# The experts' gather and scatter on GpSimd: one loop over blocks, with the next gather issued between a scatter and the wait for its landing

## The chip, the cores and the metric

The kernel runs on one core of one Trainium2 chip. The metric is the device time of one execution in microseconds. Three runs of the kernel before are shown, and one further execution was profiled. The engines are called by the profile's names: PE is TensorE, DVE is VectorE, ACT is ScalarE, POOL is GpSimd, SP is SyncE, which issues the plain transfers.

## The reference, cut to what matters

One layer of a streaming encoder runs on 1024 prompt tokens and 32 sample tokens: a combined projection, two attention branches, gates, an output projection and a layer norm. Then comes the part that is changed, a mixture of experts with 32 experts, of which each token takes two:

```python
dest = pad_start[e_s] + jnp.arange(n_assign) - cnt_start[e_s]
xb = jnp.zeros((n_blocks * MOE_BLOCK, h.shape[1]), h.dtype).at[dest].set(h[tok_s])
block_e = jnp.minimum(jnp.searchsorted(pad_end, jnp.arange(n_blocks) * MOE_BLOCK, side='right'), N_EXPERTS - 1)

def expert_block(a):
    xblk, e = a
    return (jax.nn.silu(xblk @ lp['w_gate'][e]) * (xblk @ lp['w_up'][e])) @ lp['w_down'][e]

yb = lax.map(expert_block, (xb.reshape(n_blocks, MOE_BLOCK, -1), block_e)).reshape(n_blocks * MOE_BLOCK, -1)
return jax.ops.segment_sum(yb[dest] * w_s[:, None].astype(yb.dtype), tok_s, num_segments=n_tok)
```

The assignments are sorted by expert and cut into blocks of 128 rows of one expert. The matrices of one expert are 1024 x 512 (gate), 1024 x 512 (up) and 512 x 1024 (down).

## The kernel before, in words

**Tiling.** After the router has counted, the program knows how many blocks each expert has. Every expert gets at least one, so that the code can walk the experts in order; with these inputs there are 40 blocks, eight of them second blocks of an expert. Each block is 128 rows of 1024 numbers. Float32 products are made of three matmuls on split operands (high by high, low by high, high by low), and each operand is split into a high part (ACT rounds it) and a rest (DVE subtracts).

**One block on PE** (`block_mm`, lines 1017 to 1050): gate and up for the first half of the hidden width, then for the second (L1030 to L1032); then `turn_x(b + 1)`, eight transposes of the **next** block's rows `xg` into PSUM (L1008); then the down product of this block (L1046 to L1048). `turn_x` waits for the gather: `x_got` must be `16 * b + 16`.

**The weights.** SP loads each expert's weights in six transfers of 1 MB, each as soon as the last block of the expert before has used that part (`w_used`). ACT rounds them (L1325) and DVE makes the rest (L1823). Both do it in thirds, in a fixed order between the small steps of a block. On ACT the order at a new expert is: first third, `drain_y` (L1318, two copies of the previous block's result from PSUM to `yb`), second third, and so on. `drain_y` waits for the end of the down product and for the semaphore `give_step`.

**POOL** carries the data that depend on the routing. Both helpers issue an indirect transfer:

- `fetch(b)` gathers block b's rows into the single buffer `xg`. It reads the block's column number (`value_load`), waits until the gather before has landed and until `turn_x(b - 1)` has emptied `xg` (`xb_tr`), writes a one-element tick (`step`, L2051), copies 128 row numbers into `idx` (L2060), ticks again and issues (L2063). The ticks order instructions that depend on each other through semaphores.
- `give(b)` scatters the result of block b - 1 from the single buffer `yb` to `y_rows`. It copies 128 destinations (L2075), waits for `drain_y` (`y_read`), ticks (`settle`, L2070), issues (L2079), **waits until the scatter has landed** (`y_sent`), and ticks again. This second tick raises `give_step`, which lets ACT's next `drain_y` overwrite `yb`.

The loop goes over experts: `fetch(b + 1)`, `give(b)`, and then an inner loop with the same pair for further blocks of the expert. Since an engine works in order, `fetch` of the next round is not reached until the scatter of this round has landed. Both transfers use the software-driven DMA queue q0; SP's transfers use q1.

After the last block POOL issues the last `give`. SP then waits for all scatters (`y_sent`), reads the rows back, and a second layer norm ends the program.

Of the kernel before, what the change touches and what calls it, by code (L numbers as in the profile page):

```python
# [14 lines left out]
ALU = mybir.AluOpType  # L15
# [4 lines left out]
I32 = mybir.dt.int32  # L20
U32 = mybir.dt.uint32

P = 128
# [11 lines left out]
NE, NG, EPG = 32, 4, 8  # L35
DE = 512
MAXBLK = NE + 2 * LIVE // P
# [101 lines left out]
NTL = NT + 1  # L139
# [30 lines left out]
def build(nc, io):  # L170
    with ExitStack() as ctx:
        def sem(name):
            return ctx.enter_context(nc.semaphore(name))
# [26 lines left out]
        ps = ctx.enter_context(nc.psum_tensor("ps", [P, 8, 512], F32))  # L200
# [14 lines left out]
        r = Region(base)  # L215
# [3 lines left out]
        r = Region(work)  # L219
# [12 lines left out]
        r = Region(rope_at)  # L232
# [13 lines left out]
        r = Region(work)  # L246
# [15 lines left out]
        def u_at(c):  # L262
            return nc_u + c * TOK * 4
# [7 lines left out]
        r = Region(u_at(C_KA))  # L271
        back = [r.take("back0", [P, 2, LIVE])]
        assert r.at <= u_at(C_QB)
        r = Region(work)
# [5 lines left out]
        r = Region(base)  # L280
# [4 lines left out]
        r = Region(base + 2 * 4 * KD * D)  # L285
# [4 lines left out]
        r = Region(nc_u)  # L290
# [16 lines left out]
        r = Region(after_m)  # L307
# [31 lines left out]
        total = r.take("total", [P, NE])  # L339
        reach = r.take("reach", [P, NE])  # L340
        blk = r.take("blk", [P, 4])
        blk_i = r.take("blk_i", [1, 2, MAXBLK + 1], I32)
        last_blk = r.take("last_blk", [1, NE], I32)
        rank = r.take("rank", [P, NTL, 2])
        spare = r.take("spare", [P, 1])
# [2 lines left out]
        r = Region(base)  # L348
        e_raw, e_hi, e_lo = map(list, zip(*[r.split(f"we{n}", [P, GC]) for n in range(2)]))
        assert r.at <= nc_u  # L350
        r = Region(work)
# [3 lines left out]
        r = Region(moe_small)  # L355
# [14 lines left out]
        r = Region(ring_at)  # L370
        pad = r.take("pad", [P, NCOL])
        rank_f = r.take("rank_f", [P, NCOL])
        r = Region(ring_at + 2 * 4 * NCOL)
        dest = r.take("dest", [P, NCOL], I32)

        r = Region(base)
        yg = [r.take(f"yg{n}", [P, 2, D]) for n in range(YB)]
        on = [r.take(f"on{n}", [P, D]) for n in range(2)]
        r = Region(work)
# [6 lines left out]
        def s(name):  # L386
            if name not in sems:
                sems[name] = sem(name)
            return sems[name]
# [1016 lines left out]
        def _(dve):  # L1406
# [419 lines left out]
            for t in range(NTL):  # L1826
# [20 lines left out]
                if t == 7:  # L1847
# [37 lines left out]
                                     op1=ALU.add).then_inc(s("blk_done"), 1)  # L1885
            rest_third(0, 0, range(2))
            dve.wait_ge(s("blk_tr"), 1)
            dve.tensor_copy(blk_i[:, 0, :], ps[0:1, 1, 0:MAXBLK + 1]).then_inc(s("plan"), 1)
            dve.tensor_scalar(blk_i[:, 1, :], ps[0:1, 1, P:P + MAXBLK + 1], float(NE * NTL - 1), None, ALU.min
                              ).then_inc(s("plan"), 1)  # L1890
            rest_third(0, 0, range(2, 4))

# [59 lines left out]
            with dve.Fori(1, NE) as e:  # L1952
                b = dve.value_load(last_blk[0:1, bass.ds(e - 1, 1)], min_val=0, max_val=MAXBLK - 2) + 1
# [3 lines left out]
            nb = dve.value_load(last_blk[0:1, NE - 1:NE], min_val=NE - 1, max_val=MAXBLK - 1) + 1  # L1957
            dve.wait_ge(s("w_used2"), nb * 2)
            for t in ORDER:
                M = rows_of(t)  # L1960
                last = dve.tensor_scalar(share[0:M, t, 0:M], ident[0:M, 0:M], prow[0:M, t, 1:2], None, ALU.mult)
# [41 lines left out]
        def _(pool):  # L2003
# [9 lines left out]
            for dst, src in ((ident_r, ident), (mask_r, blkmask)):  # L2013
                last = pool.tensor_copy(dst[:], src)
# [33 lines left out]
            def step(count):  # L2048

                pool.wait_ge(s("pool_step"), count)  # L2050
                pool.tensor_tensor(tick[:, 0:1], zero[0:1, :], zero[0:1, :], ALU.add).then_inc(s("pool_step"), 1)  # L2051

            def fetch(b, first):

                if not first:
                    column = pool.value_load(blk_i[0:1, 1, bass.ds(b, 1)], min_val=0, max_val=NE * NTL - 1)
                    pool.wait_ge(s("x_got"), 16 * b)
                    pool.wait_ge(s("xb_tr"), b)
                    step(2 * b)
                    pool.tensor_copy(idx[:, 0:1], tokens[:, bass.ds(column, 1)]).then_inc(s("idx_set"), 1)  # L2060
                pool.wait_ge(s("idx_set"), b + 1)
                step(2 * b + 1)
                pool.indirect_dma_start(out=xg[:], out_offset=None, in_=h_rows,  # L2063
                                        in_offset=bass.IndirectOffsetOnAxis(ap=idx[:, 0:1], axis=0)
                                        ).then_inc(s("x_got"), 16)

            def settle(count):

                pool.wait_ge(s("give_step"), count)
                pool.tensor_tensor(tick[:, 1:2], zero[0:1, :], zero[0:1, :], ALU.add).then_inc(s("give_step"), 1)  # L2070

            def give(done):

                column = pool.value_load(blk_i[0:1, 1, bass.ds(done - 1, 1)], min_val=0, max_val=NE * NTL - 1)
                pool.tensor_copy(idx[:, 1:2], dest[:, bass.ds(column, 1)]).then_inc(s("idx_out"), 1)  # L2075
                pool.wait_ge(s("idx_out"), done)
                pool.wait_ge(s("y_read"), 2 * done)
                settle(2 * done - 1)
                pool.indirect_dma_start(out=y_rows, out_offset=bass.IndirectOffsetOnAxis(ap=idx[:, 1:2], axis=0),  # L2079
                                        in_=yb[:], in_offset=None).then_inc(s("y_sent"), 16)  # L2080
                pool.wait_ge(s("y_sent"), 16 * done)
                settle(2 * done)

            def more_blocks(e, b):
                last = pool.value_load(last_blk[0:1, bass.ds(e, 1)], min_val=0, max_val=MAXBLK - 1)
                with pool.If(last > b):
                    with pool.Fori(b + 1, last + 1) as more:
                        fetch(more + 1, False)
                        give(more)

            fetch(0, True)
            pool.wait_ge(s("tokens"), 1)
            pool.wait_ge(s("plan"), 3)
            fetch(1, False)
            pool.wait_ge(s("dests"), 1)
            more_blocks(0, 0)
            with pool.Fori(1, NE) as e:
                b = pool.value_load(last_blk[0:1, bass.ds(e - 1, 1)], min_val=0, max_val=MAXBLK - 2) + 1
                fetch(b + 1, False)
                give(b)  # L2100
                more_blocks(e, b)
            nb = pool.value_load(last_blk[0:1, NE - 1:NE], min_val=NE - 1, max_val=MAXBLK - 1) + 1

            give(nb)

            for j in range(NTL):
                v = mv[j % 2][0:rows_of(ORDER[j])]
# [93 lines left out]
```

## Time and profile before

| | us |
|---|---|
| median of three runs | 1733.33 |
| lowest and highest | 1728.21 and 1743.21 |
| the profiled execution | 1728.43 |
| its span, first to last instruction | 1726.6 |

| engine | busy us | share of the span |
|---|---|---|
| PE | 1665.7 | 96% |
| DVE | 1099.2 | 64% |
| ACT | 824.2 | 48% |
| POOL | 317.3 | 18% |

The experts take from about 934 us to 1675 us. Busy shares are means over the whole span, so the work around the change is read from windows between two starts of `turn_x`, one per block. The mean granted clock of the span is 0.983.

### The profile page before, as it was taken

To read this page: it belongs to the slowest core of one execution; us is meant where nothing else is said; L and a number is where in the kernel's file an instruction comes from. 1 tells how busy PE (TensorE), PEld (TensorE's weight loads), DVE (VectorE), ACT (ScalarE), POOL (GpSimd) and SP (SyncE) were. 2 spreads that over 40 slices of the span, in tenths; PEclk is the share of its full clock that TensorE was granted. 3 is DMA by queue.
4 is the path that set the end of the run, shared out by engine and by line. 5 is a ranking of instruction groups with operands and counts; after the bars stand their busy time and mean duration, and the time that the engine had idled before them with its cause. 6 is when DMAs were issued, how large, how long until landed. Compare 5 with 4: busy or idle time off the path is not lost. (4 is left out here: it accounts for less than half of the span.)

```text
span 1726.6 us, 28243 instructions
## 1 busy us (share of the span) xinstructions
PE 1665.7 (96%) x9680; PEld 1390.1 (81%) x9681; DVE 1099.2 (64%) x1719; ACT 824.2 (48%) x1291; POOL 317.3 (18%) x383
## 2 busy tenths in 40 slices
PE   8999999999999999999996999999999999999986
PEld 8988888788888889998874778888878888887762
DVE  3466655455555454553578874559886568698867
ACT  3134443433434334111222764458785557587853
POOL 0000000000000000002431332223343223233431
PEclk9999999999999998999996999999999999999998
DMA  5110010411111112533225976669997668899967
GB/s 194 37 44 26 26 37 13 175 44 41 50 50 51 50 47 109 190 129 109 78 93 189 366 266 233 262 247 391 408 398 280 252 255 331 330 399 408 395 224 283
DMA packets 64332, 324.19 MB, mean 188 GB/s; under 512 B 7681, under 2 KB 14465, under 8 KB 37601
## 3 DMA queue, kind: packets, MB, share of 16 engines
q1 hardware_dynamic: 52592, 280.68, 42.7%
q0 software_dynamic: 11664, 42.47, 7.0%
q8 instruction: 52, 0.85, 0.2%
q14 instruction: 24, 0.19, 0.0%
HBM read 280.36 MB, written 42.76 MB: 187 GB/s over the span
## 5 line engine op out<-in xcount | busy, mean ns | idle before, releaser
L1823 DVE TENSOR_TENSOR we_lo<-we_raw,we_hi 128x1024 fp32r<-128x1024 f32 x384 | 449.4, 1219 | 31.8 <-ACT we_hi L1325 27.9
L1325 ACT ACTIVATE we_hi<-we_raw 128x1024 fp32r<-128x1024 f32 x384 | 378.0, 1052 | 44.1 <-issue 39.3
L1030 PE MATMUL ps<-we_hi,xb_hi 128*128 128x512 f32 x640 | 256.7, 401 | 3.4 <-DVE xb_lo L1904 2.0
L1032 PE MATMUL ps<-we_hi,xb_lo 128*128 128x512 f32 x640 | 250.8, 392 | 0.0
L1031 PE MATMUL ps<-we_lo,xb_hi 128*128 128x512 f32 x640 | 249.7, 390 | 0.0
L554 PE MATMUL ps<-xT_hi,win_hi 128*128 128x358 f32 (+1 forms) x432 | 145.4, 337 | 8.3 <-DVE win_lo L1423 8.3
L1030 PEld LDWEIGHTS ps<-we_hi,xb_hi 128*128 128x128 f32 x640 | 120.5, 188 | 34.9 <-DVE we_lo L1823 9.4
L1032 PEld LDWEIGHTS ps<-we_hi,xb_lo 128*128 128x128 f32 x640 | 120.4, 188 | 26.3
L555 PE MATMUL ps<-xT_lo,win_hi 128*128 128x358 f32 (+1 forms) x432 | 141.5, 327 | 0.0
L556 PE MATMUL ps<-xT_hi,win_lo 128*128 128x358 f32 (+1 forms) x432 | 141.1, 327 | 0.0
L1031 PEld LDWEIGHTS ps<-we_lo,xb_hi 128*128 128x128 f32 x640 | 120.8, 189 | 23.6
L845 PE MATMUL ps<-xT_hi,wgate_hi 128*128 128x352 f32 x384 | 135.9, 354 | 0.5 <-DVE wgate_lo L1582 0.5
L1046 PE MATMUL ps<-we_hi,hb_hi 128*128 128x512 f32 x320 | 136.1, 425 | 0.0
L1048 PE MATMUL ps<-we_hi,hb_lo 128*128 128x512 f32 x320 | 126.7, 396 | 0.0
L1047 PE MATMUL ps<-we_lo,hb_hi 128*128 128x512 f32 x320 | 126.2, 394 | 0.0
L847 PE MATMUL ps<-xT_hi,wgate_lo 128*128 128x352 f32 x384 | 125.2, 326 | 0.0
L846 PE MATMUL ps<-xT_lo,wgate_hi 128*128 128x352 f32 x384 | 125.1, 326 | 0.0
L2070 POOL TENSOR_TENSOR tick<-const 1x1 f32<-1x1 f32 x80 | 45.8, 573 | 332.9 <-DMA y_rows<-yb,idx 243.8
L1898 DVE TENSOR_TENSOR hid<-sg,ps 128x256 f32<-128x256 f32 x80 | 33.5, 418 | 101.2 <-ACT sg L1329 101.2
L1197 ACT ACTIVATE wt<-ps 128x768 f32<-128x768 f32 (+2 forms) x60 | 47.9, 799 | 94.4 <-PE ps L776 93.8
L1560 DVE TENSOR_TENSOR_SCAN left<-keep 128x384 f32<-128x384 f32 (+5 forms) x66 | 51.5, 821 | 64.2 <-ACT keep L1185 33.5
L554 PEld LDWEIGHTS ps<-xT_hi,win_hi 128*128 128x128 f32 x432 | 81.9, 189 | 9.1 <-DVE win_lo L1423 8.0
(343 smaller groups left out, 3233.7 us busy)
## 6 DMA issues: line engine op xcount, KB each, us to landing
we_raw<-w_moe SPq DMA_DIRECT2D x192, 1024.0 KB, 7.3
win_raw<-w_u SPq DMA_DIRECT2D x18, 512.0 KB, 3.5
gates<-sgt SPq DMA_DIRECT2D x48, 176.0 KB, 1.8
back<-gates SPq DMA_DIRECT2D x8, 1056.0 KB, 5.9
wgate_raw<-w_mix SPq DMA_DIRECT2D x16, 512.0 KB, 3.6
yg<-y_rows SPq DMA_DIRECT2D x8, 1024.0 KB, 8.8
xT_raw<-xT SPq DMA_DIRECT2D x8, 536.0 KB, 8.3
kvb<-U SPq DMA_DIRECT2D x1, 4224.0 KB, 15.6
```

Of the source, the lines that this page charges most:

```text
L554: pe.matmul(o, whi[n][:, kk, :], xh[:, kk, a:b], start=kk == 0, stop=False)
L555: pe.matmul(o, whi[n][:, kk, :], xl[:, kk, a:b], start=False, stop=False)
L556: return pe.matmul(o, wlo[n][:, kk, :], xh[:, kk, a:b], start=False, stop=kk == KD - 1)
L845: pe.matmul(o, ghi[c % 2][:, k, :], xh[:, k, cols], start=k == 0, stop=False, skip_group_check=True)
L1030: pe.matmul(o, xb_hi[:, k, :], e_hi[half][:, c], start=k == 0, stop=False)
L1031: pe.matmul(o, xb_hi[:, k, :], e_lo[half][:, c], start=False, stop=False)
L1032: last = pe.matmul(o, xb_lo[:, k, :], e_hi[half][:, c], start=False, stop=k == KD - 1)
L1046: pe.matmul(o, hb_hi[:, k, :], e_hi[2][:, cols], start=k == 0, stop=False)
L1047: pe.matmul(o, hb_hi[:, k, :], e_lo[2][:, cols], start=False, stop=False)
L1048: last = pe.matmul(o, hb_lo[:, k, :], e_hi[2][:, cols], start=False, stop=k == 3)
L1325: act.activation(e_hi[n][:, c], e_raw[n][:, c], ACT.Copy).then_inc(s("d_hi" if n == 2 else "e_hi"), 1)
L1823: dve.tensor_tensor(e_lo[n][:, c], e_raw[n][:, c], as_f32(e_hi[n][:, c]), ALU.subtract).then_inc(s("d_split" if n == 2 else "e_split"), 1)
```

## The change

POOL's two nested loops become one loop over blocks. `give` is cut in two: the part up to the issue keeps its name, and the wait for the landing with its tick is called `given`. `fetch(2)` moves ahead of the loop, and inside the loop `fetch(b + 2)` stands between the two parts. At the end one gather more is issued than before (`fetch(nb + 1)`), for which the table of columns gets one entry more. Nothing is changed on PE, ACT and SP, and on DVE only the width of two copies of that table (49 columns to 50).

```diff
-            dve.tensor_copy(blk_i[:, 0, :], ps[0:1, 1, 0:MAXBLK + 1]).then_inc(s("plan"), 1)
-            dve.tensor_scalar(blk_i[:, 1, :], ps[0:1, 1, P:P + MAXBLK + 1], float(NE * NTL - 1), None, ALU.min
+            dve.tensor_copy(blk_i[:, 0, :], ps[0:1, 1, 0:MAXBLK + 2]).then_inc(s("plan"), 1)
+            dve.tensor_scalar(blk_i[:, 1, :], ps[0:1, 1, P:P + MAXBLK + 2], float(NE * NTL - 1), None, ALU.min
                               ).then_inc(s("plan"), 1)
...
                 settle(2 * done - 1)
                 pool.indirect_dma_start(out=y_rows, out_offset=bass.IndirectOffsetOnAxis(ap=idx[:, 1:2], axis=0),
                                         in_=yb[:], in_offset=None).then_inc(s("y_sent"), 16)
+
+            def given(done):
+
                 pool.wait_ge(s("y_sent"), 16 * done)
                 settle(2 * done)
-
-            def more_blocks(e, b):
-                last = pool.value_load(last_blk[0:1, bass.ds(e, 1)], min_val=0, max_val=MAXBLK - 1)
-                with pool.If(last > b):
-                    with pool.Fori(b + 1, last + 1) as more:
-                        fetch(more + 1, False)
-                        give(more)
 
             fetch(0, True)
             pool.wait_ge(s("tokens"), 1)
             pool.wait_ge(s("plan"), 3)
             fetch(1, False)
             pool.wait_ge(s("dests"), 1)
-            more_blocks(0, 0)
-            with pool.Fori(1, NE) as e:
-                b = pool.value_load(last_blk[0:1, bass.ds(e - 1, 1)], min_val=0, max_val=MAXBLK - 2) + 1
-                fetch(b + 1, False)
+            fetch(2, False)
+            nb = pool.value_load(last_blk[0:1, NE - 1:NE], min_val=NE - 1, max_val=MAXBLK - 1) + 1
+            with pool.Fori(1, nb) as b:
                 give(b)
-                more_blocks(e, b)
-            nb = pool.value_load(last_blk[0:1, NE - 1:NE], min_val=NE - 1, max_val=MAXBLK - 1) + 1
-
+                fetch(b + 2, False)
+                given(b)
             give(nb)
+            pool.wait_ge(s("x_got"), nb * 16 + 32)
+            step(nb * 2 + 4)
```

POOL's instructions in the loop over experts before, from a scatter's issue (`DMA y_rows`) onward; `y_sent` counts landed scatters:

```order
L2079 DMA y_rows<-yb,idx 2240x1024
L2081 REGISTER_ALU
L2070 TENSOR_TENSOR tick<-const 1x1 [waits give_step,y_sent]
L2085 ISA
L2085 TENSOR_LOAD last_blk
L2085 ISA x2
L2086 COMPARE_AND_BRANCH
L2087 UNCONDITIONAL_BRANCH
L2087 ISA
L2056 TENSOR_LOAD blk_i
L2056 ISA x2
L2057 ISA
```

The tick that waits for the landing stands two rows behind the issue; the branches of the two loops and the load of the next gather's column come after it.

The same place in the changed loop, from the scatter's issue to the second tick ahead of the gather; `xb_tr` counts emptied `xg` buffers:

```order
L2079 DMA y_rows<-yb,idx 2240x1024
L2056 ISA
L2056 TENSOR_LOAD blk_i
L2056 ISA x2
L2057 ISA
L2050 REGISTER_ALU [waits xb_tr,x_got]
L2051 TENSOR_TENSOR tick<-const 1x1 [waits pool_step]
L2060 ISA
L2060 COPY idx<-tokens 128x1
L2061 REGISTER_ALU
L2050 REGISTER_ALU [waits idx_set]
L2051 TENSOR_TENSOR tick<-const 1x1 [waits pool_step]
```

Between the scatter and the gather's own instructions no wait for `y_sent` is left; what POOL waits for here is `xb_tr`.

The rows that follow in the changed loop, from the gather's issue (`DMA xg`) to the head of the next round:

```order
L2063 DMA xg<-h_rows,idx 128x1024
L2084 REGISTER_ALU
L2070 TENSOR_TENSOR tick<-const 1x1 [waits give_step,y_sent]
L2094 ISA
L2094 COMPARE_AND_BRANCH
L2074 ISA
L2074 TENSOR_LOAD blk_i
```

The tick that waits for the landing, and that ACT's `drain_y` waits for, now stands behind the gather's issue, and one branch closes the loop.

## Rows read from the trace of the kernel before

**Rows 1.** The page, chain that ended last, its shares of the span by line:

```profile
PE ps L1030 7%; PE ps L1032 7%; PE ps L1031 7%; PE ps L1046 4%; PE ps L1048 3%; PE ps L1047 3%; DMA xg<-h_rows,idx 2%; PE ps L1008 2%; PE ps L1014 1%; POOL y_rows L2079 1%; DMA y<-on 1%; POOL idx L2060 0%; POOL tick L2070 0%; DVE on L1988 0%; DVE yg L1979 0%
```

**Rows 2.** Waits of PE and POOL: who for whom, total us, times, longest:

```profile
PE ps L1008 <- DMA xg<-h_rows,idx: 10.2, 6, 3.3
...
POOL tick L2070 <- DMA y_rows<-yb,idx: 243.8, 40, 9.2
...
POOL tick L2051 <- issue: 81.3, 25, 19.5
POOL tick L2051 <- PE ps L1008: 73.8, 16, 5.9
```

**Rows 3.** Windows between `turn_x` starts: us, busy of PE PEld DVE ACT POOL, PEclk, DMA:

```profile
987.90:1009.56 21.66, 18.34 (x85) 14.40 (x83) 19.29 (x22) 15.53 (x22) 7.75 (x8) 0.99 0.99 381
1009.56:1029.06 19.50, 19.47 (x84) 15.90 (x85) 13.81 (x16) 14.18 (x19) 5.61 (x9) 0.93 0.66 253
...
1209.00:1227.16 18.16, 18.16 (x85) 14.55 (x84) 16.50 (x19) 14.85 (x21) 7.03 (x8) 1.00 1.01 411
...
1245.30:1265.11 19.81, 18.34 (x86) 14.41 (x84) 17.43 (x21) 15.52 (x22) 8.66 (x8) 1.00 1.01 411
...
1590.20:1609.54 19.34, 18.30 (x85) 14.41 (x84) 17.00 (x21) 15.53 (x22) 8.67 (x8) 1.00 1.01 404
1609.54:1628.30 18.76, 18.33 (x85) 14.56 (x85) 16.19 (x18) 14.73 (x20) 7.75 (x8) 1.00 0.98 384
1628.30:1649.04 20.74, 18.35 (x84) 14.53 (x85) 18.32 (x21) 14.98 (x21) 7.86 (x8) 1.00 1.01 389
```

**Rows 4.** Timeline of POOL, 1237 to 1260 us: start, duration, instruction, [idle before]:

```profile
1237.60 2.03 POOL L2079 DMA_INDIRECT y_rows<-yb,idx  x1 [0.16 <-POOL tick L2070]
1248.47 0.36 POOL L2070 TENSOR_TENSOR tick<-const 1x1 f32<-1x1 f32 x1 [8.84 <-DMA y_rows<-yb,idx]
1251.02 1.16 POOL L2051 TENSOR_TENSOR tick<-const 1x1 f32<-1x1 f32 x1 [2.19 <-issue]
...
1254.61 1.81 POOL L2063 DMA_INDIRECT xg<-h_rows,idx  x1 [0.15 <-issue]
...
1258.23 1.81 POOL L2079 DMA_INDIRECT y_rows<-yb,idx  x1 [0.16 <-POOL tick L2070]
```

**Rows 5.** Timeline of PE, the transposes of three blocks:

```profile
933.66 1.97 PE L1008 MATMUL ps<-const,xg 128*128 128x128 f32 x8 [1.57 <-DMA xg<-h_rows,idx]
...
1209.00 1.03 PE L1008 MATMUL ps<-const,xg 128*128 128x128 f32 x8
...
1265.11 1.09 PE L1008 MATMUL ps<-const,xg 128*128 128x128 f32 x8 [1.47 <-DMA xg<-h_rows,idx]
```

**Rows 6.** Timeline of POOL, a gather that the transposes released, 1030 to 1034 us:

```profile
1030.33 1.13 POOL L2051 TENSOR_TENSOR tick<-const 1x1 f32<-1x1 f32 x1 [4.34 <-PE ps L1008]
...
1033.40 1.00 POOL L2063 DMA_INDIRECT xg<-h_rows,idx  x1 [0.47 <-issue]
```

**Rows 7.** Timeline of ACT, `drain_y` of the block at 1209 us:

```profile
1217.31 1.06 ACT L1318 ACTIVATE yb<-ps 128x512 f32<-128x512 f32 x2
```

**Rows 8.** The gather's line: issue durations, min/median/max ns; issue to landing:

```profile
L2063 POOL DMA_INDIRECT xg<-h_rows,idx x41: 986/1553/2032, 929.0 to 1658.4; - x41
...
DMA to landing us min/median/max: 4.2/6.5/10.7
```

**Rows 9.** Timeline of POOL, the last two scatters, 1662 to 1680 us:

```profile
1662.02 1.80 POOL L2079 DMA_INDIRECT y_rows<-yb,idx  x1 [0.16 <-POOL tick L2070]
1666.22 1.14 POOL L2070 TENSOR_TENSOR tick<-const 1x1 f32<-1x1 f32 x1 [2.40 <-DMA y_rows<-yb,idx]
...
1676.27 1.00 POOL L2079 DMA_INDIRECT y_rows<-yb,idx  x1 [0.28 <-POOL tick L2070]
1679.86 0.18 POOL L2070 TENSOR_TENSOR tick<-const 1x1 f32<-1x1 f32 x1 [2.58 <-DMA y_rows<-yb,idx]
```

**Rows 10.** The page, costliest groups: DVE's rests of the weights:

```profile
L1823 DVE TENSOR_TENSOR we_lo<-we_raw,we_hi 128x1024 fp32r<-128x1024 f32 x384 | 449.4, 1219 | 31.8 <-ACT we_hi L1325 27.9
```

More of the change, by code:

```diff
@@ L341, in build @@
         blk = r.take("blk", [P, 4])
-        blk_i = r.take("blk_i", [1, 2, MAXBLK + 1], I32)
+        blk_i = r.take("blk_i", [1, 2, MAXBLK + 2], I32)
         last_blk = r.take("last_blk", [1, NE], I32)
```

## The prediction

> **What bounds the kernel now.** I read the chain of waits first. Most of it is PE, but in the experts it also runs through the gather's landing (2% of the span, some 35 us) and the scatter's issue (1%) [rows 1]. That is a lead, not a price: a chain goes back through whatever ended last, also where the next engine lost little by it.
>
> The price stands in the list of waits. PE's transposes waited for a gather six times, 10.2 us in all [rows 2]. One of the six is the first block's (1.57 us, rows below), with nothing ahead of it that the change moves. On POOL the same list shows the pattern: 40 waits for a scatter's landing, 243.8 us together, and of the ticks that open a gather only 16 were released by PE's transposes, while 25 came at a moment when nothing was left to wait for, so late [rows 2]. In 25 blocks or so POOL is behind, and in five PE notices it.
>
> The windows by block say how much it notices. A block with new weights takes 18.16 us when PE is not held up, and PE is then busy for all of it; five windows are longer and PE's busy time in them hardly is, except where the granted clock fell [rows 3]. So PE bounds the experts, and POOL's round holds it up now and then.
>
> Why POOL falls behind is read from one round [rows 4]. Scatter issued at 1237.60, landing seen at 1248.47 (10.87 us), the next gather's first tick at 1251.02 (2.55 us for branches and loads), gather issued at 1254.61, next scatter issued at 1258.23. From scatter to scatter that is 20.63 us against PE's 18.16. Each such round costs POOL some 2 us of a lead; when it is used up, PE waits, as at 1265.11, 10.50 us after the gather's issue [rows 4, 5].
>
> **The change, part by part.**
>
> *The gather no longer waits for the scatter.* It then waits for the transposes, as the 16 do now. From the end of the transposes (1029.06 by the window's end, plus 1.03 us) it took 0.24 us to the first tick and 3.31 us to the issue [rows 3, 5, 6]. When DVE is busy POOL's small steps are slower: 3.59 us from tick to issue [rows 4]. So the gather is issued at most 3.83 us after the transposes; it lands at most 10.7 us later [rows 8], at 14.5 us; the next transposes start 18.16 - 1.03 = 17.1 us after the last ones ended. 2.6 us are left in the worst mix, so I cost the gather at nothing and expect all five waits to go.
>
> Each is worth its window over 18.16 us [rows 3]: 21.66 gives 3.50, 19.81 gives 1.65, 19.34 gives 1.18, 18.76 gives 0.60, 20.74 gives 2.58. Behind the longest of these the granted clock was 0.93 in the next window: part of it ran at 1.2 instead of 2.4 GHz after PE had stood still, and that window is 1.34 longer. Together **10.85 us**. The least I can defend is the idle time alone, 10.2 - 1.57 = 8.6 us [rows 2, 5]; the most is a little more than the sum.
>
> *The settle tick now stands behind the gather.* ACT's `drain_y` waits for it, and behind `drain_y` ACT has the second third of the weights. The gather's instructions take 1254.61 + 1.81 - 1251.02 = 5.40 us when slow [rows 4]; with 0.24 us ahead and a slow tick of 1.14 us [rows 9] behind, the tick ends 6.8 us after the transposes. `drain_y` started at 1217.31, that is 7.28 us after the transposes ended at 1210.03 [rows 5, 7]. The slack is 0.5 us; nothing is charged, but this is the thinnest margin of the change. The scatter itself is no later than that: issued in the block before, it has landed about when the transposes end.
>
> *Loads and branches go* (the 2.55 us [rows 4]). POOL's round becomes at most 10.87 us to the landing, 2.55 us of loop, and 3.6 us from there to the next scatter, 17.0 us: shorter than PE's block, so POOL stops falling behind. That time is off the path and counts nothing.
>
> *One gather more, 512 KB, at the end.* It stands ahead of the last scatter on POOL and on the same queue. A scatter right behind a gather landed in 4.20 us, the last one with nothing ahead in 3.59 us [rows 9]: 0.6 us on the path, since the read-back waits for it. POOL must also get through the slow gather and tick first (6.8 us after the last transposes, then loop exit and a copy), about when `drain_y` ends; I add 0.6 us. Bounds: 0, and 7.1 us if the scatter had to wait out a slow gather of 10.7 us instead of 3.59. I take 1.2 us, since the weights no longer load then and 4.20 is the nearest row. The final wait for that gather lies beside the read-back. DVE's two copies grow by one column: nothing.
>
> **The sum** is -10.85 + 1.2 = -9.7 us on the profiled execution's 1728.4, so 1718.8. The median of the three runs is 4.9 above that execution, the lowest run beside it. I put the forecast a little over the sum, at **1720 us**, with a range of its own of 1714 to 1726. Against the median that is 0.8% less; about 1% is what a measurement of this kernel can tell from no change, so it counts as within 1%.
>
> **The rivals.**
>
> *The transfers are the bound behind PE (0.12).* A block with new weights moves 6 x 1.049 MB of weights, 0.52 MB in and 0.52 MB out, 7.34 MB. At 18.16 us that is 404 GB/s, and the share of the DMA engines reads 0.98 to 1.01 in such windows [rows 3]. If they can't hold this over a run of such blocks, the weights come late where the gather did: the five waits go and return on the weights, for about 1728 us. Against it: the window at 18.16 us moved 411 GB/s [rows 3]. The Trainium skill, "DMA: Bandwidth & Descriptors", Specifications, gives about 358 GB/s of HBM for a core; by it such a block would need an estimated 20.5 us, the waits on the gather would be a symptom and the change would gain nothing. The trace disagrees: 381 to 411 GB/s in all six windows with new weights through their whole length.
>
> *The settle tick comes too late (0.06).* This one ends slower. The mechanism is `drain_y` on ACT held by POOL, then the second third of the weights late, then PE's second half. It decides where the tick ends later than 7.28 us after the transposes, 0.5 us beyond the slowest steps seen; from there each microsecond costs up to one in each of the 31 blocks that open an expert. One microsecond beyond, less what the change gains, gives 1728 - 10 + 31 = 1750 us. Speaking for it: POOL's steps now fall right behind the transposes while DVE works through weights, at 1219 ns apiece [rows 10], and the slow gathers took 2.03 us to issue where the fast took 0.99 [rows 8]. The Trainium skill, "SBUF — State Buffer", SBUF: two separate sides, says that some DVE operations lock POOL out of a shared port and so starve a gather of descriptors, with an example of 620 ns growing to about 3100. By that rule with its factor of five, 0.99 us would become an estimated 5 us and the tick would be late by more than 2 us. The rows show a factor of two in the worst case.
>
> *The other runs hold more of these waits than the profiled one (0.20).* The runs shown reach 1743.21. POOL's lead is lost by small differences in landing times, and one long wait costs clock as well. If the 5 to 15 us over the profiled execution are such waits, the changed kernel sheds them too, and the gain against the median passes 1%: about 1714 us.
>
> *The change doesn't reach the wait* would need the gather late although issued 3.8 us after the transposes. Its slowest landing leaves 2.6 us, so I give this the 0.02 that is left, with no change in time.
>
> **The numbers.** The forecast has 0.60. Faster by over 1% is the third rival and a little of the forecast's lower edge, 0.22. Slower by over 1% is the second rival, 0.06. Within 1% is the rest, 0.72. The range reaches from 1709 (the third rival with the gains a little larger) to 1733 (the transfers, or a settle tick that eats the gain), and leaves out the second rival and the ends.
>
> **What would show it.** Right: in the experts' windows no block over 18.3 us; no wait of the transposes for a gather except the first block's; nearly all ticks that open a gather released by the transposes; the granted clock at 1.00 from 1009 us on; 18.16 us and some 404 GB/s held through the run of single blocks at the end. Wrong: waits on the weights in the same windows (transfers), or ACT's `drain_y` released by POOL's tick and PE waiting for the rests of the weights (settle), or a last scatter that takes 6 us or more to land (the extra gather).

## The result, and the profile after

The changed kernel takes **1717.99 us** (median of 9 runs, 1714.71 to 1718.89). The kernel before, in the same session, takes 1731.89 (9 runs, 1723.87 to 1743.21). The ratio is **0.9928, 95% interval 0.9903 to 0.9952**: 0.7% faster, clear of the noise, and inside the 1% that the forecast called no measurable change. The forecast was 1720, the range 1709 to 1733. The spread fell too: 19 us between the lowest and the highest run before, 4 us after.

The profiled execution after took 1717.99 us, span 1716.2 (before: 1728.4 and 1726.6). Three cuts show where the 10.4 us of the span went: up to the first block's transposes, from there to the last block's, and the rest. Windows of the kernel before (columns: stretch, length; busy time of PE, PEld, DVE, ACT, POOL with instruction counts; granted clock, DMA share, GB/s):

```profile
933.66:1667.22 733.56, 721.56 (x3334) 582.37 (x3335) 549.17 (x633) 491.89 (x688) 246.36 (x316) 0.99 0.83 322
1667.22:1726.60 59.38, 40.51 (x107) 18.39 (x105) 38.87 (x52) 18.06 (x43) 8.79 (x14) 0.88 0.59 228
```

The same two windows of the kernel after, then one block with new weights near the end, then the last nine blocks:

```profile
934.09:1656.49 722.40, 719.13 (x3334) 581.77 (x3335) 548.81 (x633) 491.65 (x688) 225.43 (x315) 1.00 0.84 327
1656.49:1716.20 59.71, 40.62 (x107) 18.53 (x105) 38.87 (x52) 18.05 (x43) 11.22 (x18) 0.86 0.60 235
...
1620.21:1638.35 18.14, 18.14 (x86) 14.56 (x85) 16.51 (x19) 14.85 (x21) 6.51 (x8) 1.00 1.01 421
...
1493.13:1656.49 163.36, 163.36 (x757) 131.06 (x756) 148.59 (x163) 133.63 (x181) 58.66 (x72) 1.00 0.99 395
```

The experts became 733.56 - 722.40 = 11.16 us shorter; the tail 0.33 longer, the experts start 0.43 later. In the last nine blocks PE is busy for all of 163.36 us: 18.15 us a block, where the kernel before had windows of 19.34, 18.76 and 20.74 [rows 3]. The low-clock window behind 1009 us is gone with the pause that stood ahead of it.

Waits of PE and POOL after (engine, line, whom it waited for: total us, times, longest), to be compared with [rows 2]; then the gather's line (issue ns min/median/max, and landing), to be compared with [rows 8]:

```profile
PE ps L1008 <- DMA xg<-h_rows,idx: 1.6, 1, 1.6
```

```profile
POOL tick L2051 <- PE ps L1008: 299.2, 40, 9.2
```

```profile
L2063 POOL DMA_INDIRECT xg<-h_rows,idx x42: 980/995/1209, 929.3 to 1660.8; - x42
...
DMA to landing us min/median/max: 4.2/7.7/9.6
```

PE waits for a gather once, the first block's. Forty ticks that open a gather are now released by PE's transposes (16 before), the list has no wait of POOL for a scatter's landing any more, and the gather's issue takes 0.995 us in the median where it took 1.553. The last is a hint that the prediction passed over: the gather not only comes sooner, its own steps are shorter. The way to the landing did not become shorter: its median went from 6.5 to 7.7 us.

One round of POOL after (start, duration, instruction, idle before and its releaser); the transposes of this block ran from 1186.27 to 1187.30:

```profile
1187.53 1.13 POOL L2051 TENSOR_TENSOR tick<-const 1x1 f32<-1x1 f32 x1 [6.97 <-PE ps L1008]
1188.61 1.18 POOL L2060 COPY idx<-tokens 128x1 int32 x1
1189.95 0.18 POOL L2051 TENSOR_TENSOR tick<-const 1x1 f32<-1x1 f32 x1 [0.16 <-POOL idx L2060]
1190.60 0.99 POOL L2063 DMA_INDIRECT xg<-h_rows,idx  x1 [0.47 <-issue]
1191.62 0.18 POOL L2070 TENSOR_TENSOR tick<-const 1x1 f32<-1x1 f32 x1
```

DVE and ACT beside it:

```profile
1187.39 2.35 DVE L1823 TENSOR_TENSOR we_lo<-we_raw,we_hi 128x1024 fp32r<-128x1024 f32 x2
1189.66 0.42 DVE L1910 TENSOR_TENSOR hb_lo<-ps,hb_hi 128x256 fp32r<-128x256 f32 x1
1190.00 1.28 DVE L1904 TENSOR_TENSOR xb_lo<-ps,xb_hi 128x512 fp32r<-128x512 f32 x2
1191.87 1.23 DVE L1823 TENSOR_TENSOR we_lo<-we_raw,we_hi 128x1024 fp32r<-128x1024 f32 x1 [0.59 <-ACT we_hi L1325]
```

```profile
1194.59 1.06 ACT L1318 ACTIVATE yb<-ps 128x512 f32<-128x512 f32 x2
```

Two things are to be seen. The settle tick (L2070, 1191.62) ends 4.5 us after the transposes, and `drain_y` begins 7.29 us after them: the slack is 2.8 us. And POOL's first two steps take 1.13 and 1.18 us beside two of DVE's weight subtractions, while the same kind of tick takes 0.18 and the gather's issue 0.99 beside L1910 and L1904, whose first operand is PSUM.

Now the same place in the kernel before, DVE around the slow gather of [rows 4]:

```profile
1248.70 0.42 DVE L1910 TENSOR_TENSOR hb_lo<-ps,hb_hi 128x256 fp32r<-128x256 f32 x1
1249.03 1.28 DVE L1904 TENSOR_TENSOR xb_lo<-ps,xb_hi 128x512 fp32r<-128x512 f32 x2
1250.91 9.39 DVE L1823 TENSOR_TENSOR we_lo<-we_raw,we_hi 128x1024 fp32r<-128x1024 f32 x8 [0.60 <-ACT we_hi L1325]
```

At 1250.91 DVE begins eight weight subtractions without a pause, and at 1251.02 POOL's first tick for the gather begins. From that tick to the end of the gather's issue POOL takes 5.40 us [rows 4]. This gave **theory A**: the gather was late because its steps met this run of subtractions. The rival, **theory B**, is the prediction's own: it was late because it queued behind the scatter's landing on an engine whose whole round was too long.

The last scatter of the kernel after, for the prediction's last term, against the 1676.27 row of [rows 9]:

```profile
1665.54 1.01 POOL L2079 DMA_INDIRECT y_rows<-yb,idx  x1 [0.28 <-DMA xg<-h_rows,idx]
```

### The profile page after: what moved, and what is told of

Read it like the earlier page. It is cut to its first block and busy times, and to the rows that moved or that the text cites. A ratio compares the mean times of both kernels' runs of the same rounds, so it can differ in the third digit from the quotient of the medians.

```text
span 1716.2 us, 27931 instructions
## 1 busy us (share of the span) xinstructions
PE 1663.9 (97%) x9680; PEld 1390.5 (81%) x9681; DVE 1099.1 (64%) x1719; ACT 823.8 (48%) x1291; POOL 298.7 (17%) x387
## 5 line engine op out<-in xcount | busy, mean ns | idle before, releaser
L1823 DVE TENSOR_TENSOR we_lo<-we_raw,we_hi 128x1024 fp32r<-128x1024 f32 x384 | 449.5, 1220 | 30.2 <-ACT we_hi L1325 26.5
L1325 ACT ACTIVATE we_hi<-we_raw 128x1024 fp32r<-128x1024 f32 x384 | 377.9, 1052 | 44.4 <-issue 39.3
```

Source lines behind the costliest of these rows:

```text
L1325: act.activation(e_hi[n][:, c], e_raw[n][:, c], ACT.Copy).then_inc(s("d_hi" if n == 2 else "e_hi"), 1)
L1823: dve.tensor_tensor(e_lo[n][:, c], e_raw[n][:, c], as_f32(e_hi[n][:, c]), ALU.subtract).then_inc(s("d_split" if n == 2 else "e_split"), 1)
```

## The experiments

The runs were taken in three further sessions, in which the kernel before took 1727.5, 1730.4 and 1730.6 us in the median. Each ratio below is to the kernel before of its own session; the kernel after is not among their runs.

### The two halves of the change

The change makes the loop flat (no loads and branches of two nested loops) and puts the gather ahead of the wait for the landing. Each was done alone. First the flat loop with the old order, written against the kernel after:

```diff
-            fetch(2, False)
             nb = ...
             with pool.Fori(1, nb) as b:
+                fetch(b + 1, False)
                 give(b)
-                fetch(b + 2, False)
                 given(b)
             give(nb)
-            pool.wait_ge(s("x_got"), nb * 16 + 32)
-            step(nb * 2 + 4)
```

> One flat loop over blocks on GpSimd, but in the old order: gather, scatter, wait for the scatter's landing; no gather more at the end. Before, the way from the landing's tick to the next gather's first tick took 2.55 us and held two loads and several branches that the flat loop doesn't have; about 1.3 us of it should go. My theory (the landing ahead of the gather is the cause): GpSimd's self-timed round falls from 19.3 to 20.6 us to about 18.0 to 19.3 us, on both sides of TensorE's 18.16, so part of the waits stays, above all the longest one near 1009 us: 3 to 7 of the 10.9 us are still lost, 1720 to 1725 us against some 1731 of before. Rival (loads and branches were the cause): no wait of the transposes for a gather is left except the first block's, 1717 to 1718 us.

Measured: **1717.32 us** (6 runs, 1716.21 to 1719.2), ratio to before 0.9948 (0.9927 to 0.9968). The expected time was missed: the flat loop alone brings the whole gain, though POOL still waits for the landing in every block. Its waits for the scatter, and one gather late in the program (turn_x at 1620.52):

```profile
POOL tick L2070 <- DMA y_rows<-yb,idx: 234.2, 39, 8.3
```

```profile
1622.85 1.20 POOL L2070 TENSOR_TENSOR tick<-const 1x1 f32<-1x1 f32 x1 [8.01 <-DMA y_rows<-yb,idx]
1624.01 0.18 POOL L2051 TENSOR_TENSOR tick<-const 1x1 f32<-1x1 f32 x1
...
1625.13 1.00 POOL L2063 DMA_INDIRECT xg<-h_rows,idx  x1 [0.47 <-issue]
```

```profile
1626.12 1.23 DVE L1823 TENSOR_TENSOR we_lo<-we_raw,we_hi 128x1024 fp32r<-128x1024 f32 x1 [0.58 <-ACT we_hi L1325]
```

The waits for the landing are nearly as long as before (234.2 us in 39 waits against 243.8 in 40 in [rows 2]). But the gather's first tick comes 1.16 us after the landing tick's start, not 2.55, and the gather is issued by 1626.13, just as DVE's subtractions start again.

The other half: the new order inside the old nested loops, with their loads and branches.

```diff
-            with pool.Fori(1, nb) as b:
+            def round_of(b):
                 give(b)
                 fetch(b + 2, False)
                 given(b)
+            def more_blocks(e, b):
+                last = pool.value_load(last_blk[0:1, bass.ds(e, 1)], ...)
+                with pool.If(last > b):
+                    with pool.Fori(b + 1, last + 1) as more:
+                        round_of(more)
+            more_blocks(0, 0)
+            with pool.Fori(1, NE) as e:
+                b = pool.value_load(last_blk[0:1, bass.ds(e - 1, 1)], ...) + 1
+                round_of(b)
+                more_blocks(e, b)
```

> The new order (scatter issued, next gather issued, then the wait for the landing) with the old nested loops over experts and their loads and branches kept. My theory: the branches stand behind the landing's tick, where GpSimd has several us to spare before the next drain; the time is that of the changed kernel, 1716 to 1719 us, and no gather is waited for but the first. Rival (loads and branches were the cause): half or more of the 10.9 us comes back, 1723 us or more.

Measured: **1716.87 us** (6 runs), ratio 0.9945 (0.9925 to 0.9966), as expected. PE waits for a gather once, the first block's:

```profile
PE ps L1008 <- DMA xg<-h_rows,idx: 1.3, 1, 1.3
```

So either half is enough, and the two do not add. This contradicts theory B as far as it says that the wait for the landing has to go.

### How far, and where, the delay has to be

One register load in POOL's loop takes about half a microsecond (below: 14 of them, 6.67 us). Three were put into the flat loop with the old order, once ahead of the gather and once behind it. POOL's round holds the same work in both; what differs is the moment of the gather's steps.

```diff
             with pool.Fori(1, nb) as b:
                 fetch(b + 1, False)
                 give(b)
                 given(b)
+                for _ in range(3):
+                    pool.value_load(last_blk[0:1, 0:1], ...)
```

> The flat loop in the old order with three register loads (0.48 us each, 1.44 us in all) between the landing's tick and the next gather's first tick, about what the flat loop had saved; no branches. Theory A (GpSimd's small steps fall on VectorE's run of eight weight subtractions, which starts 4.5 us after the transposes end, and so grow from 2.1 to 3.5 to 5.4 us): the gather's steps are slow in most single-expert blocks, GpSimd's rounds are 19 to 20.6 us, 6 to 13 us are lost: 1723 to 1731 us. Rival B (only the length of the loads counts): the round is that of the flat loop plus 1.44 us, GpSimd still waited 2.7 to 3.9 us per round for the drain there, so nothing is lost: 1717 to 1719 us.

Measured: **1733.32 us** (10 runs, 1726.14 to 1743.84), ratio 1.0023 (0.9996 to 1.005). That is 2 us above the upper end of what theory A expected. The whole gain is lost, and the spread of the kernel before is back. PE's waits, one gather, and DVE beside it:

```profile
PE ps L1008 <- DMA xg<-h_rows,idx: 14.5, 9, 2.3
```

```profile
1247.78 0.18 POOL L2070 TENSOR_TENSOR tick<-const 1x1 f32<-1x1 f32 x1 [8.80 <-DMA y_rows<-yb,idx]
1250.57 0.45 POOL L2051 TENSOR_TENSOR tick<-const 1x1 f32<-1x1 f32 x1 [2.61 <-issue]
1250.96 1.18 POOL L2060 COPY idx<-tokens 128x1 int32 x1
1252.31 0.98 POOL L2051 TENSOR_TENSOR tick<-const 1x1 f32<-1x1 f32 x1 [0.16 <-POOL idx L2060]
1253.44 1.81 POOL L2063 DMA_INDIRECT xg<-h_rows,idx  x1 [0.15 <-issue]
```

```profile
1249.75 2.36 DVE L1823 TENSOR_TENSOR we_lo<-we_raw,we_hi 128x1024 fp32r<-128x1024 f32 x2 [0.89 <-ACT we_hi L1325]
```

The gather's first tick starts 0.82 us after the subtractions begin, and its steps take 4.68 us.

The same with one load in place of three:

> The same with one load, 0.48 us: the gather's steps start about 3 us after the transposes end and finish ahead of VectorE's run at 4.5 us or just run into it. Theory A: no wait but the first block's, 1717 to 1719 us, the steps 2.1 to 3 us long. Rival B: the same time, the steps unchanged at 2.1 us. Rival C (every 0.48 us costs its share of the 10.9 us, some 3.6 us): 1721 us.

Measured: **1717.14 us** (6 runs), ratio 0.9924 (0.9894 to 0.9954). Only the first block waits. Both theories expected this time; what the run excludes is a cost in proportion to the delay. POOL, then DVE:

```profile
1242.57 0.29 POOL L2070 TENSOR_TENSOR tick<-const 1x1 f32<-1x1 f32 x1 [7.80 <-DMA y_rows<-yb,idx]
1244.25 0.18 POOL L2051 TENSOR_TENSOR tick<-const 1x1 f32<-1x1 f32 x1 [1.40 <-issue]
...
1245.37 1.00 POOL L2063 DMA_INDIRECT xg<-h_rows,idx  x1 [0.47 <-issue]
```

```profile
1246.06 1.23 DVE L1823 TENSOR_TENSOR we_lo<-we_raw,we_hi 128x1024 fp32r<-128x1024 f32 x1 [0.60 <-ACT we_hi L1325]
```

And the three loads moved behind the gather:

```diff
             with pool.Fori(1, nb) as b:
                 fetch(b + 1, False)
+                for _ in range(3):
+                    pool.value_load(last_blk[0:1, 0:1], ...)
                 give(b)
                 given(b)
```

> The flat loop in the old order with the same three register loads, but behind the gather's issue, ahead of the scatter's part; GpSimd's round holds as much work as in the run with three loads ahead of the gather, which lost all that the flat loop had gained. Theory A (it is the moment at which the gather's steps meet VectorE's run of weight subtractions): the gather starts as early as in the flat loop, its steps take 2.1 us, and the loads lie in the wait for the drain: no wait but the first block's, 1717 to 1719 us. Rival B (the length of GpSimd's round): as with the loads ahead, 1726 us or more.

Measured: **1717.39 us** (5 runs), ratio 0.9919 (0.989 to 0.9947), as theory A expected. POOL, then DVE:

```profile
1242.93 1.18 POOL L2070 TENSOR_TENSOR tick<-const 1x1 f32<-1x1 f32 x1 [8.05 <-DMA y_rows<-yb,idx]
1244.07 0.18 POOL L2051 TENSOR_TENSOR tick<-const 1x1 f32<-1x1 f32 x1
...
1245.19 1.00 POOL L2063 DMA_INDIRECT xg<-h_rows,idx  x1 [0.47 <-issue]
```

```profile
1246.20 1.22 DVE L1823 TENSOR_TENSOR we_lo<-we_raw,we_hi 128x1024 fp32r<-128x1024 f32 x1 [0.61 <-ACT we_hi L1325]
```

The same three loads cost 16 us ahead of the gather and nothing behind it, where POOL waits for `drain_y` anyway. So neither the amount of work in POOL's round nor the wait for the landing decides. Plain delay isn't enough either: with one load every gather but the first lands at least 3.46 us before the transposes that need it start, and two loads more delay its first tick by 1.11 us (2.79 - 1.68). The rest came from the slower steps, and from a longer way to the landing: 8.8 to 10.8 us from issue in the eight blocks past the first that waited with three loads, at most 9.9 with one. Of that only the slower issue (1.8 to 2.0 instead of 1.0 us) is accounted for. Put together, from the rows above (one block of each kernel, so the phases hold for these blocks; the median issue is over all gathers):

| kernel | landing tick to first tick, us | first tick against DVE's run | first tick to end of issue, us | median issue, us | median time, us |
|---|---|---|---|---|---|
| before [rows 4, 8] | 2.55 | 0.11 after its start | 5.40 | 1.553 | 1731.9 |
| flat, 3 loads ahead | 2.79 | 0.82 after | 4.68 | 1.488 | 1733.3 |
| flat, 1 load ahead | 1.68 | 1.81 ahead | 2.12 | 1.002 | 1717.1 |
| flat, 3 loads behind | 1.14 | 2.13 ahead | 2.12 | 0.999 | 1717.4 |
| flat | 1.16 | 2.11 ahead | 2.12 | 0.999 | 1717.3 |
| after | no such wait | 4.34 ahead | 4.06 | 0.995 | 1718.0 |

In the old order a first tick 1.68 us behind the landing tick cost nothing, and one 2.55 us behind it cost the whole gain; the threshold lies between. A gather whose steps are through when DVE's run starts needs 2.12 us. One that falls wholly into it needs 2.3 to 3.6 us more (the kernel before and the one with three loads ahead); then, in the old order, the scatter behind it is issued later, lands later, and the next gather meets the run again. The kernel before shows it in its last run of single blocks, up to the wait at 1649.04: the first tick comes 3.04, 3.78, 3.77, 4.09, 4.16, 4.66, 5.41 and 6.43 us after the transposes end, and tick to end of issue takes 2.12, 2.88, 2.89, 3.70, 3.64, 5.40, 4.66 and 5.00 us; PE waits in the last three. The round of [rows 4] took 20.63 us against PE's 18.16 (the prediction's figures); the loop keeps itself late until PE waits. The changed order stands so far ahead that even its 4.06 us (two single subtractions met) do no harm.

### The settle tick

Five register loads, and then fourteen, between the gather and the tick for which `drain_y` waits:

```diff
                 give(b)
                 fetch(b + 2, False)
+                for _ in range(5):      # and 14
+                    pool.value_load(last_blk[0:1, 0:1], ...)
                 given(b)
```

> The changed kernel with five more register loads between the gather's issue and the tick for the scatter's landing, about 0.5 us each, 2.5 us in all. In the changed kernel the tick starts about 4.3 us after the transposes end and the drain on ScalarE at 7.3 us. My theory: 2.5 us fit in the 2.8 us of room, no more than 3 us in all are lost: 1717 to 1721 us. Rival (the tick is already what the drain waits for): up to 2.5 us in each of 31 blocks, up to 1790 us.

Measured: **1718.89 us** (10 runs, 1718.17 to 1720.0), as expected: 0.9 us over the kernel after, 2.0 over the new order in the nested loops of the same session. In the profile the tick starts 1.95 us later (1193.57) and still ends before `drain_y`:

```profile
1193.57 0.94 POOL L2070 TENSOR_TENSOR tick<-const 1x1 f32<-1x1 f32 x1 [1.73 <-issue]
```

Nine drains wait for the tick (37.9 us in all); in the kernel after, nine wait for PE instead (36.4 us).

> The changed kernel with fourteen more register loads at that place, about 7 us. The tick then ends some 11.5 us after the transposes, 4.2 us after ScalarE would drain. My theory of the slower rival's price: VectorE's rests of the second third come late and TensorE waits in its second half; about 1 us is absorbed, so 2 to 3.5 us in each of 31 blocks that open an expert: 1780 to 1825 us, with TensorE's waits on the rests of the weights and the drain released by GpSimd's tick. Rival (the drain's lateness is hidden since its result is needed a block later): 1717 to 1722 us.

Measured: **1831.51 us** (one run), a little above the expected range. POOL's tick, ACT's `drain_y`, PE's waits, and two windows between `turn_x` starts:

```profile
1260.02 1.00 POOL L2063 DMA_INDIRECT xg<-h_rows,idx  x1 [0.47 <-issue]
1267.68 0.18 POOL L2070 TENSOR_TENSOR tick<-const 1x1 f32<-1x1 f32 x1 [6.67 <-issue]
```

```profile
1267.90 1.08 ACT L1318 ACTIVATE yb<-ps 128x512 f32<-128x512 f32 x2 [3.83 <-POOL tick L2070]
```

```profile
PE ps L1030 <- DVE we_lo L1823: 76.4, 31, 3.0
```

```profile
1277.34:1300.35 23.01, 20.07 (x86) 15.61 (x84) 16.61 (x19) 14.97 (x21) 4.99 (x8) 0.93 0.85 317
1255.66:1277.34 21.68, 18.68 (x86) 14.39 (x85) 16.35 (x19) 15.00 (x21) 5.02 (x8) 1.00 0.91 341
```

This is the chain of the prediction's second rival, link by link: POOL's tick, `drain_y` 3.83 us late, the rests of the weights late, PE waiting 31 times, as many as there are blocks that open an expert. The price is 1831.5 - 1718.0 = 113.5 us, 3.7 us a block; in the first window it is more than the delay, and there the granted clock was 0.93: after PE's pauses part of the block ran at 1.2 instead of 2.4 GHz.

### The kernel before once more

The unchanged kernel before was profiled again, to see whether the waits sit in the same places.

> The kernel before once more, for a second trace of it. My theory: the scatter of its times, 1720 to 1743 us, is the number and size of the waits of the transposes for a gather; the span less the windows' excess over 18.16 us comes to 1715 to 1717 us in this execution too, whatever its time. Rival: the excess is the same 10 to 12 us and the time differs elsewhere (transfers, clock).

Measured: 1729.6 us (one run), span 1727.8. PE's waits for a gather:

```profile
PE ps L1008 <- DMA xg<-h_rows,idx: 8.2, 6, 2.7
```

The long windows were others, of 19.66, 19.45, 19.28, 18.90 and 21.06 us and one of 19.54 at a lower granted clock; over 18.16 they make about 8.9 us. Taken off the span, that leaves 1718.9, more than was expected and 2.7 over the span of the kernel after: some 2 us lay in the tail, which took 61.67 us here, 59.38 in the other profile of this kernel and 59.71 after. So the waits change place and size from run to run, which fits a threshold. That they make the spread of the times is not shown: both profiled executions lie near 1729 us, and none near 1740 was profiled. For it speaks that the two kernels with such waits spread by 18 and 19 us and the others by 2 to 6. Most of the tail's difference is PE's busy time, 42.19 us against 40.51, at a granted clock of 0.84 against 0.88; what brought the clock down is open.

### Are the transfers next?

One more transfer of 1 MB per expert on SP's queue, from memory to memory, and nobody waits for it before the end:

```diff
+                sp.dma_start(waste[bass.ds(e, 1)]..., io["w_moe"][bass.ds(e, 1), 0, :, 0:2048]...
+                             ).then_inc(s("wasted"), 16)
```

> The changed kernel with one more transfer of 1 MB per expert on SyncE's queue, from memory to memory, behind the expert's weights. A single-expert block then moves 8.39 instead of 7.34 MB; at 18.16 us that is 462 GB/s, where the highest window so far shows 421. Theory 'the transfers are next behind TensorE': the weights come late and blocks grow to the time that some 405 to 421 GB/s need, 19.9 to 20.7 us, 1.8 to 2.5 us in each of 23 blocks: 1755 to 1780 us. Rival (there is room): 1717 to 1722 us.

Measured: **1751.0 us** (4 runs), ratio to before 1.0111 (1.0073 to 1.015), somewhat under the expected range but on its side. A stretch of 150 us in the experts, then ACT's wait for the weights and PE's longest wait in the experts (line numbers are six higher in this kernel, so L1331 is L1325):

```profile
1530.00:1680.00 150.00, 139.18 (x633) 108.61 (x632) 124.25 (x136) 113.85 (x151) 39.26 (x64) 1.00 1.01 424
```

```profile
ACT we_hi L1331 <- DMA we_raw<-w_moe: 85.2, 106, 3.0
PE ps L1052 <- DVE hb_lo L1916: 15.3, 18, 0.9
```

The weights come late: ACT waits for them 106 times, 85.2 us in all, where the kernel after has 4 such waits and 5.1 us. PE is no longer always busy (139.18 of 150 us), and the DMA engines move 424 GB/s for the whole stretch. The share reads 1.01, as it did at 404 and 421 GB/s: a share of 1 alone does not say that nothing more goes through. The kernel after needs 404 in a block with new weights (the prediction's figure), so with this mix of transfers they are the next bound, some 5% above PE's pace, and not the present one.

### A version that beats both

After the change ACT pauses 1.44 us at the end of each expert: it loads the expert's last block from memory and decides on a branch, and only then rounds the first third of the next weights, which opens DVE's run. The load can stand earlier, in cover:

```diff
                 if not first:
                     round_third(2, e, range(2))
+                    last = act.value_load(last_blk[0:1, bass.ds(e, 1)], ...)
                 round_h(0, b)
...
-                last = act.value_load(last_blk[0:1, bass.ds(e, 1)], ...)
+                if last is None:
+                    last = act.value_load(last_blk[0:1, bass.ds(e, 1)], ...)
```

> The changed kernel with one register load of ScalarE (the number of the expert's last block) moved from the end of a block, where it stands ahead of the next expert's first third of the weights, to an earlier place where ScalarE waits anyway. Single-expert blocks take 18.16 us against 17.87 of blocks that open no expert; the 0.29 us are TensorE's wait for the first rest of the weights, which ScalarE's way through loads and branches (1.42 us) makes late. Theory: 0.48 us earlier takes that wait away, 17.9 us a block: 23 blocks by 0.29 plus 8 by 0.13 us, 6 to 8 us less than the changed kernel, 1709 to 1712 us. Rival (VectorE's rests of the block's rows come late anyway): no change, 1716 to 1719 us.

Measured: **1713.29 us** (6 runs, 1710.75 to 1716.21), ratio to before 0.9893 (0.9861 to 0.9924): the fastest kernel here, but 4.7 us under the kernel after (in another session) and not the 6 to 8 expected. In the profiled executions the experts took 719.17 us, against 722.40 in the kernel after. A block with new weights, then ACT's first rounding in the kernel after and in this run:

```profile
1184.86:1202.87 18.01, 18.01 (x86) 14.60 (x85) 16.44 (x19) 14.90 (x21) 7.70 (x8) 1.00 1.01 418
```

```profile
1190.78 3.90 ACT L1325 ACTIVATE we_hi<-we_raw 128x1024 fp32r<-128x1024 f32 x4 [1.44 <-issue]
...
1188.77 3.91 ACT L1325 ACTIVATE we_hi<-we_raw 128x1024 fp32r<-128x1024 f32 x4 [0.84 <-issue]
```

The pause is 0.84 us instead of 1.44, and the block 18.01 instead of 18.14 to 18.17. PE's rows show it busy for the whole window in both kernels, so what went is time inside its matmul rows; by which path was not tried.

## Why the prediction was right, point by point

- **The five waits.** Forecast -10.85 us from them; measured -11.16 between the first and the last transposes, with all five gone and the low-clock window too (granted clock 1.00 from 1006.50 to 1024.62 us). Right in sign, size and place. One block over 18.3 us is left, the second, which takes 19.38 us in both kernels.
- **The cause of the waits.** Half right. The gather was late, and POOL's round was longer than PE's. But it was the moment at which the gather's steps met DVE's run of subtractions that made it so, not the wait for the landing as such (flat loop with the old order) and not the amount of work in the round (three loads behind the gather). Of the 20.63 us of POOL's round, 3.28 are the slower steps (5.40 - 2.12); without them it would be an estimated 17.35, shorter than PE's 18.16. The prediction saw the 5.40 us and took them for a cost that the new order would also bear. The Trainium skill, "SBUF — State Buffer", SBUF: two separate sides, holds the key that was used for a rival only: a DVE operation with two operands in SBUF takes the port that it shares with GpSimd for the whole instruction, against a GpSimd instruction that reads SBUF. The trace agrees with that rule: ticks of 0.18 us beside L1910 and L1904, which have one operand in PSUM, and of 0.98 to 1.20 us beside L1823.
- **Loads and branches count nothing.** Wrong as a reason, without effect on the number. Taking them away is by itself worth the whole gain, because the 2.55 us lay ahead of the gather on a path with a threshold. The sum came out right because the two halves do not add.
- **The settle tick.** Uncharged, and rightly. The slack is 2.8 us, not 0.5: the steps behind the transposes meet two subtractions and then the PSUM operations, never the run of eight, so the slow bound of 5.40 us did not apply. Its mechanism is real and dear: 3.7 us a block when it is 3.8 us late.
- **The gather at the end.** Charged 1.2 us in two halves; the trace shows neither. The last scatter is issued 9.05 us after the last `turn_x` starts in both kernels (1676.27 - 1667.22 before, 1665.54 - 1656.49 after), so POOL's part is nothing. The queue's part is nothing too: the extra gather has landed when the scatter is issued, and the scatter lands 3.33 us after its issue, before the change 3.51. The 0.33 us by which the tail is longer is less than the 2.3 us by which it differs between two profiles of the kernel before. Without this term the sum would have been 1717.6, against 1717.99 measured.
- **The transfers as a rival.** Excluded as the bound here: 421 GB/s in a block of the kernel after and 395 through the last nine, 424 with added load. The limit that the prediction took from the Trainium skill, "DMA: Bandwidth & Descriptors", Specifications, about 358 GB/s, is not that of this case. The same page's section Bandwidth gives 425 GB/s for a 16 MB transfer by a core whose neighbour is idle, and 424 agrees with it.
- **More waits in the other runs.** Partly right: the medians differ by 13.9 us, the profiled pair by 10.4, and the spread went from 19 to 4 us. Waits that change place would explain this; no slower execution was profiled to show it.

Not shown: that DVE's run alone is the cause, since taking the run itself away was not tried; all shifts were made on POOL's side. DVE's subtractions did not become longer by it: the 384 took 1.203 to 1.231 us each before and 1.203 to 1.227 after. Whether some of them started later is open.

## What to carry to other kernels

Before taking out a wait, look at what the neighbours of the waiting engine run at the moment it is released: the same three register loads cost nothing at one place and 16 us at another, where they moved small steps into a neighbour's run. If the gap sits just beyond such a threshold, the cheapest cut ahead of it (here the loop's loads and branches) is worth as much as a new order. And run-to-run spread that one kernel has and its variants have not can point to a threshold; it is worth a second profile of the same kernel.

## What the hardware showed that was not expected

- A one-element tick on POOL takes 0.18 us, and up to 1.20 us beside DVE's 1219 ns subtractions in SBUF; an indirect transfer's issue takes 0.99 and up to 2.04 us. Four such steps in a row turn 2.12 into 5.40 us.
- A register load costs POOL some 0.35 to 0.55 us of sequencer time (14 in 6.67 us, 5 in 1.73, and one that moved the gather's first tick from 1.16 to 1.68 us), in which its row shows no busy time.
- A DMA share of 1.01 stood beside 389 GB/s [rows 3] as well as beside 424, so the rate must be read, not the share.
